# Triangular inverse of a chunked DeltaNet: the last doubling level as pairs of 64-row matmuls

## The chip, the cores and the metric

The kernel runs on 1 core of a Trainium2 chip. The metric is the device time of one launch in microseconds (us), the median of several runs. All data is fp32.

## What is computed

The reference is a two-layer encoder: a gated DeltaNet mixer, a latent attention mixer, and a mixture of experts behind each. The change is in the DeltaNet mixer. It has 8 key heads with 2 value heads each, 512 tokens, and runs the gated delta rule in both directions d (forward, and backward over flipped tokens). In each chunk it inverts a triangular matrix:

```python
a = jnp.where(strict, jnp.einsum('nbhcd,nbhsd->nbhcs', k_beta, k) * decay, 0.0)
t_inv = lax.linalg.triangular_solve(a + eye, jnp.broadcast_to(eye, a.shape),
                                    left_side=True, lower=True, unit_diagonal=True)
u = jnp.einsum('nbhcs,nbhsd->nbhcd', t_inv, v * beta[..., None])
w = jnp.einsum('nbhcs,nbhsd->nbhcd', t_inv, k_beta * jnp.exp(g)[..., None])
```

A recurrence over the chunks follows (`step` in the reference), then a norm, a gate and the output projection.

## The kernel before

The DeltaNet phase loops over the 8 key heads: `body` runs seven times in a hardware loop with the preparation of the next head woven in (`with_next`), and once more for the last head without it. A chunk is 128 tokens here, a tile of 128 x 128; there are TT = 4 tiles and two value heads h, so one fp32 bank of 128 x 512 holds the four tiles of one h.

The inverse is built by doubling. Diagonal blocks of 8 are solved first (L1027 to L1038). Then levels l = 3 to 6 merge blocks of size b = 2^l into blocks of 2b, for both directions at once: `TU[:, 0]` holds the transposed inverse T and `TU[:, 1]` the inverse U, each with a copy for direction 0 and one for direction 1, and `merged` (L287) reads them as one matrix whose column blocks alternate between the directions. At each level, for each value head h:

- TensorE makes X = A^T T (`make_x`, L550) in bank 4 + h, four 128 x 128 matmuls.
- VectorE masks the bank to the off-diagonal blocks of the level and writes it to `X` (`mask_x`, L1020), signalling `xm_ready`. `X` and `A` lie in the buffer that the profile calls `wd`.
- ScalarE copies U in merged order to `W` (L764), signalling `W_ready`.
- TensorE makes Y (`make_y`, L556, not at the last level) and V (`make_v`, L562) in banks 6 + h and 2 + h.
- VectorE subtracts them from T and U (`update`, L1025), signalling `T_ready` and `U_ready`.

Every engine follows its own instruction order, written out by hand; semaphores tie them together. TensorE puts `filler` pieces between these steps: in the loop heads 32 single matmuls of the next head's projections (L419), of which 8 stand ahead of the 8-blocks, 14 among them, and two at each of the two places of a level until they are used up; in the last head 16 pieces of the z projection. VectorE puts convolution steps (L930) and silu steps (L939) of the next head into numbered slots (`between`), four slots a level. At level 6 these are one convolution step between the two masks and one silu between the two updates.

Behind the last level TensorE runs the first quarter of the z projection (`make_z`, L503, only in the loop heads), and then the recurrence, whose first matmul L602 waits for all updates of U.

Of the kernel before, what the change touches and what calls it, by code (L numbers as in the profile page):

```python
# [7 lines left out]
ALU = mybir.AluOpType  # L8
# [4 lines left out]
P = 128  # L13
D = 1024
SEQ = 512
TT = SEQ // P
# [10 lines left out]
LEVELS, BASE = 7, 3  # L27
NL = LEVELS - BASE
# [87 lines left out]
PREPARE = [("D0", 2), ("tr0", 4), ("tr1", 5), ("tr2", 6), ("tr3", 7), ("D1", 3)]  # L116
TURN_O = [("oT0", 0), ("oT1", 1)]
PREPARE_LATE = [("kT", 2), ("qT", 3), ("KK", 2), ("KQ", 3)]


def dn_uses(with_next):
# [31 lines left out]
def delta_net(nc, t, dram):  # L153
# [4 lines left out]
    c, ps, res, xT = t["const"], t["ps"], t["res"], t["xT"]  # L158
# [5 lines left out]
    with ExitStack() as ctx:  # L164
# [12 lines left out]
        A, X = (t["wd"][:, 1, f].rearrange("p (c t n) -> p c t n", c=2, t=TT) for f in range(2))  # L177
# [11 lines left out]
        TU = sb("TU", [P, 2, 2, 2, TT, P])  # L189
        W = sb("W", [P, 2, TT, P])  # L190
# [30 lines left out]
        T_ready, U_ready = sem("T_ready"), sem("U_ready")  # L221
# [5 lines left out]
        xm_ready, W_ready = sem("xm_ready"), sem("W_ready")  # L227
# [8 lines left out]
        rows = Arrival(nc, t, sb, sem, 0)  # L236
# [144 lines left out]
        def _(pe):  # L381
# [13 lines left out]
            for n in range(8):  # L395
# [6 lines left out]
                for k in range(4):  # L402
                    mm = pe.transpose(ps[b][:, k * P:(k + 1) * P], res[:, tt, (half * 4 + k) * P:(half * 4 + k + 1) * P], ident)
# [4 lines left out]
            for tt in range(TT):  # L408
                for k in range(KD):
                    mm = pe.matmul(ps[2][:, tt * 64:(tt + 1) * 64], xT[:, k, tt * P:(tt + 1) * P], wba[:, k], start=k == 0, stop=k == KD - 1)  # L410
# [82 lines left out]
            def body(i, uses, with_next):  # L493
# [24 lines left out]
                def filler(n=1):  # L518
                    for _ in range(n):
                        if fill:  # L520
                            f, a = fill.pop(0)
                            f(*a)
# [4 lines left out]
                for m in range(7):  # L527
                    pe.wait_ge(R_ready, i * 8 + m + 1)
                    bank = begin(uses, f"B{m}", i)
# [23 lines left out]
                def make_y(l, h):  # L553
                    bank = begin(uses, f"Y{l}{h}", i)
                    for tt in range(TT):
                        mm = pe.matmul(bank[:, tt * P:(tt + 1) * P], W[:, h, tt], X[:, h, tt], start=True, stop=True)  # L556
                    done(mm, uses, f"Y{l}{h}")
# [4 lines left out]
                        mm = pe.matmul(bank[:, tt * P:(tt + 1) * P], X[:, h, tt], W[:, h, tt], start=True, stop=True)  # L562
                    done(mm, uses, f"V{l}{h}")

                for l in range(BASE, LEVELS):
                    make_x(l, 0)
                    make_x(l, 1)
                    filler(2 if with_next else 1)
                    for h in range(2):
                        pe.wait_ge(xm_ready, i * 2 * NL + 2 * (l - BASE) + h + 1)  # L570
                        pe.wait_ge(W_ready, i * 2 * NL + 2 * (l - BASE) + h + 1)
                        if l < LEVELS - 1:
                            make_y(l, h)
                        make_v(l, h)
                    filler(2 if with_next else 1)
                filler(99)

                if with_next:
# [289 lines left out]
        def _(dve):  # L868
# [8 lines left out]
            def got(uses, name, i):  # L877
                b, n = nth(uses, name, i)
                dve.wait_ge(full[b], n + 1)
                return ps[b]  # L880
# [118 lines left out]
            def body(i, uses, with_next, per):  # L999
# [15 lines left out]

                def mask_x(l, h):
                    bank = got(uses, f"X{l}{h}", i)
                    at = C_LEV + (l - BASE) * P
                    m = c[:, at:at + P].rearrange("p (o a) -> p o a", o=1).to_broadcast([P, TT, P])
                    nc.vector.tensor_tensor(X[:, h], bank[:].rearrange("p (t n) -> p t n", t=TT), m, ALU.mult).then_inc(xm_ready, 1)  # L1020

                def update(which, l, h):
                    bank = got(uses, f"{'YV'[which]}{l}{h}", i)
                    change = bank[:].rearrange("p (a e b) -> p a e b", e=2, b=1 << l)
                    nc.vector.tensor_tensor(merged(which, h, l), merged(which, h, l), change, ALU.subtract).then_inc(U_ready if which else T_ready, 1)  # L1025

# [1306 lines left out]
```

## Time and profile before

| | us |
|---|---|
| median of 3 runs | 1757.55 (1756.84 to 1757.8) |
| the profiled execution, its own time | 1760.1 |
| its span, first to last instruction | 1758.2 |
| TensorE busy (matmul) in it | 1576.9 |
| VectorE busy | 858.9 |
| ScalarE busy | 344.1 |
| GpSimd busy | 170.6 |
| mean granted TensorE clock | 0.948 |

One execution was taken by the profiler; its engines' rows give start, duration, engine, source line and tile names of each instruction. PE is TensorE's matmuls, PEld its weight loads, DVE VectorE, ACT ScalarE, POOL GpSimd, SP SyncE. An fp32 matmul of the program shows as two matmul records and two weight loads. A matmul's duration holds its latency, so the distance between starts, not the duration, is what one costs in a dense row. The 40 slices of the page are 44 us each.

### The profile page before, as it was taken

Reading aid. Unit: us, or ns where it says so; the run is one execution under the profiler, and the core shown is the slowest. Engines: PE = TensorE matmul, PEld = TensorE weight load, DVE = VectorE, ACT = ScalarE, POOL = GpSimd, SP = SyncE. Lnnn points to the kernel's source line nnn. Section 1 sums busy time; section 2 is a strip of 40 time slices with the busy share of each in tenths; the row PEclk is TensorE's granted clock in tenths of the full one; section 3 lists DMA queues with packets and bytes.
Section 4 is the critical chain, followed back from the end, with each engine's and each line's share of the span. In section 5 each row is a group of like instructions: output and inputs, shape, how many; then the busy total and the mean of one; then the engine's idle time right before and its main releaser. Section 6 shows DMA issues by size and latency. Waiting matters only on the chain. (4 is left out here: it accounts for less than half of the span.)

```text
span 1758.2 us, 20456 instructions
## 1 busy us (share of the span) xinstructions
PE 1576.9 (90%) x6926; PEld 995.4 (57%) x6926; DVE 858.9 (49%) x1768; ACT 344.1 (20%) x765; POOL 170.6 (10%) x171
## 2 busy tenths in 40 slices
PE   8899999999999999999986999937899997799990
PEld 5576685776857768577765444415555554644440
DVE  2665655656556565674566311134245557311115
ACT  2122122221212312222121111102322221111110
POOL 1201203012030120301101100020000001100002
PEclk9999999999999999999986999978899998699995
DMA  6760101101011010100510799932021133299964
GB/s 198 244 187 25 48 24 50 45 24 48 24 48 48 24 48 24 48 0 24 192 49 24 260 343 353 331 123 91 33 60 42 37 128 136 97 297 352 352 207 153
DMA packets 148743, 212.69 MB, mean 121 GB/s; under 512 B 8553, under 2 KB 120417, under 8 KB 148705
## 3 DMA queue, kind: packets, MB, share of 16 engines
q1 hardware_dynamic: 137600, 172.62, 30.3%
q10 hardware_dynamic: 6496, 22.81, 3.5%
q0 software_dynamic: 4608, 16.78, 2.6%
q8 instruction: 21, 0.34, 0.1%
q14 instruction: 18, 0.14, 0.0%
HBM read 174.96 MB, written 37.22 MB: 121 GB/s over the span
## 5 line engine op out<-in xcount | busy, mean ns | idle before, releaser
L1486 PE MATMUL bank<-wgu,moe_xgT 128*96 128x512 f32 x512 | 225.2, 592 | 4.3 <-DVE moe_xgT L1690 2.4
L419 PE MATMUL bank<-xT,wgu 128*128 128x512 f32 x448 | 210.6, 600 | 0.0
L1486 PEld LDWEIGHTS bank<-wgu,moe_xgT 128*96 128x96 f32 x512 | 80.9, 163 | 124.1 <-issue 124.1
L1690 DVE COPY moe_xgT<-bank 128x384 f32<-128x384 f32 x34 | 19.0, 558 | 209.8 <-PE bank L1474 205.6
L503 PE MATMUL bank<-wd,xT 128*128 128x256 f32 x512 | 117.7, 380 | 0.9 <-DVE res L1125 0.9
L1506 PE MATMUL bank<-wd,moe_hidT 128*96 128x512 f32 x256 | 115.3, 593 | 2.9 <-DVE moe_hidT L1698 2.9
L637 PE MATMUL bank<-wd,oT 128*128 128x512 f32 x256 | 116.3, 604 | 1.0 <-ACT oT L807 1.0
L419 PEld LDWEIGHTS bank<-xT,wgu 128*128 128x128 f32 x448 | 78.1, 191 | 63.7 <-issue 63.6
L503 PEld LDWEIGHTS bank<-wd,xT 128*128 128x128 f32 x512 | 95.7, 190 | 13.9 <-issue 1.7
L930 DVE SCALAR_TENSOR_TENSOR wgu<-bank,taps,wgu 128x510 f32<-128x510 f32 (+1 forms) x128 | 95.3, 744 | 8.6 <-ACT wgu L696 8.1
L1025 DVE TENSOR_TENSOR TU<-TU,bank 128x512 f32<-128x512 f32 x112 | 75.1, 686 | 20.5 <-PE bank L556 12.8
L637 PEld LDWEIGHTS bank<-wd,oT 128*128 128x128 f32 x256 | 48.3, 194 | 56.6 <-issue 52.2
L562 PE MATMUL bank<-W,wd 128*128 128x128 f32 x512 | 69.0, 278 | 7.1 <-DVE wd L1020 6.4
L1125 DVE TENSOR_TENSOR res<-res,bank 128x512 f32<-128x512 f32 x64 | 43.7, 686 | 56.6 <-PE bank L637 56.4
L1506 PEld LDWEIGHTS bank<-wd,moe_hidT 128*96 128x96 f32 x256 | 39.2, 163 | 54.7 <-issue 54.7
L562 PEld LDWEIGHTS bank<-W,wd 128*128 128x128 f32 x512 | 62.1, 192 | 9.8 <-DVE wd L1020 9.7
L550 PEld LDWEIGHTS bank<-TU,wd 128*128 128x128 f32 x512 | 62.0, 192 | 7.7 <-issue 6.7
L148 POOL TENSOR_TENSOR rs<-ss,masks 128x4 f32<-128x4 f32 x16 | 6.2, 387 | 616.4 <-DVE ss L1064 616.4
L550 PE MATMUL bank<-TU,wd 128*128 128x128 f32 x512 | 64.3, 278 | 0.0
L1547 ACT COPY moe_xgT<-bank 128x384 f32<-128x384 f32 x34 | 16.3, 478 | 242.8 <-PE bank L1474 208.0
L1704 DVE COPY moe_y_rows<-bank 96x512 f32<-96x512 f32 x32 | 22.0, 687 | 82.3 <-PE bank L1506 82.3
L1020 DVE TENSOR_TENSOR wd<-bank,masks 128x512 f32<-128x512 f32 x64 | 44.1, 689 | 36.7 <-PE bank L550 34.9
(308 smaller groups left out, 2468.3 us busy)
## 6 DMA issues: line engine op xcount, KB each, us to landing
wgu<-moe_w_gate SPq DMA_DIRECT2D x32, 1024.0 KB, 10.2
wgu<-moe_w_up SPq DMA_DIRECT2D x32, 1024.0 KB, 12.3
wd<-moe_w_down SPq DMA_DIRECT2D x32, 1024.0 KB, 5.8
wgu<-dn_w_in SPq DMA_DIRECT2D x32, 512.0 KB, 3.8
slots_y<-moe_y_rows ACTq DMA_DIRECT2D x32, 384.0 KB, 6.4
slots_x<-gains SPq DMA_DIRECT2D x1, 9984.0 KB, 39.2
moe_x_rows<-slots_x ACTq DMA_DIRECT2D x26, 384.0 KB, 7.7
wd<-dn_w_in SPq DMA_DIRECT2D x8, 1024.0 KB, 5.2
```

Source lines behind the costliest of these rows:

```text
L419: mm = pe.matmul(bank[:], wqkv[:, ct, k], xT[:, k], start=k == 0, stop=k == KD - 1)
L503: mm = pe.matmul(bank[:, (n % 2) * 256:(n % 2) * 256 + 256], xT[:, k, tt * P:(tt + 1) * P], wz[:, k], start=k == 0, stop=k == KD - 1)
L550: mm = pe.matmul(bank[:, tt * P:(tt + 1) * P], A[:, h, tt], merged(0, h, l, tt), start=True, stop=True)
L562: mm = pe.matmul(bank[:, tt * P:(tt + 1) * P], X[:, h, tt], W[:, h, tt], start=True, stop=True)
L637: mm = pe.matmul(bank[:], oT[:, h, tt], wo[:, h, half * 512:(half + 1) * 512], start=h == 0, stop=h == 1)
L930: ins = nc.vector.scalar_tensor_tensor(out=conv[:, ct, lo:hi], in0=bank[:, lo + d:hi + d], scalar=w[:, j:j + 1], in1=conv[:, ct, lo:hi], o ...
L1020: nc.vector.tensor_tensor(X[:, h], bank[:].rearrange("p (t n) -> p t n", t=TT), m, ALU.mult).then_inc(xm_ready, 1)
L1025: nc.vector.tensor_tensor(merged(which, h, l), merged(which, h, l), change, ALU.subtract).then_inc(U_ready if which else T_ready, 1)
L1125: nc.vector.tensor_tensor(y, y, bank[:], ALU.add).then_inc(y_ready, 1)
L1486: mm = pe.matmul(ps[2][0:CAP], xgT[:, r, k], wgu[:, r, k].rearrange("p a f -> p (a f)"), start=k == 0, stop=k == KD - 1)
L1506: mm = pe.matmul(ps[4 + half][0:CAP], hidT[:, f], wd[:, r, f, half * 512:(half + 1) * 512], start=f == 0, stop=f == 1)
L1704: nc.vector.tensor_copy(y_rows[:, r, 512:1024], ps[5][0:CAP]).then_inc(y_ready[1], 1)
```

## The change

At level 6 the blocks are 64 wide, and of each direction only one corner of a tile is missing. The change makes just that corner. X and V of the last level become 16 matmuls of 64 rows x 64 columns each (weights 64 x 128) instead of 8 per product of 128 x 128, alternating between the two directions: direction 0 reads partitions 0 to 63 and writes bank 4 (X) or 2 (V), direction 1 reads 64 to 127 and writes bank 5 or 3. A bank now belongs to a direction and holds both value heads, eight groups of 64 columns. The mask becomes a copy of 64 partitions, and the update of U touches the corner alone. X waits for all updates of T of level 5, V for both copies and both parts of W.

```diff
--- before.py
+++ after.py
@@ -116,6 +116,9 @@
 PREPARE = [("D0", 2), ("tr0", 4), ("tr1", 5), ("tr2", 6), ("tr3", 7), ("D1", 3)]
 TURN_O = [("oT0", 0), ("oT1", 1)]
 PREPARE_LATE = [("kT", 2), ("qT", 3), ("KK", 2), ("KQ", 3)]
+
+
+HALVES = slice(0, P // 2), slice(P // 2, P)
 
 
 def dn_uses(with_next):
@@ -562,17 +565,40 @@
                         mm = pe.matmul(bank[:, tt * P:(tt + 1) * P], X[:, h, tt], W[:, h, tt], start=True, stop=True)
                     done(mm, uses, f"V{l}{h}")
 
-                for l in range(BASE, LEVELS):
+                def last_x():
+                    l = LEVELS - 1
+                    pe.wait_ge(T_ready, i * (2 * NL - 2) + (l - BASE) * 2)
+                    banks = [ps[uses.at[f"X{l}{h}"][0]] for h in range(2)]
+                    for n in range(2 * TT):
+                        for d, rows in enumerate(HALVES):
+                            mm = pe.matmul(banks[d][:, n * 64:n * 64 + 64], A[rows, n // TT, n % TT], TU[rows, 0, d, n // TT, n % TT, rows], start=True, stop=True)
+                            if n == 2 * TT - 1:
+                                done(mm, uses, f"X{l}{d}")
+
+                def last_v():
+                    l = LEVELS - 1
+                    pe.wait_ge(xm_ready, (i + 1) * 2 * NL)
+                    pe.wait_ge(W_ready, (i + 1) * 2 * NL)
+                    banks = [ps[uses.at[f"V{l}{h}"][0]] for h in range(2)]
+                    for n in range(2 * TT):
+                        for d, rows in enumerate(HALVES):
+                            mm = pe.matmul(banks[d][:, n * 64:n * 64 + 64], X[rows, n // TT, n % TT], W[rows, n // TT, n % TT, rows], start=True, stop=True)
+                            if n == 2 * TT - 1:
+                                done(mm, uses, f"V{l}{d}")
+
+                for l in range(BASE, LEVELS - 1):
                     make_x(l, 0)
                     make_x(l, 1)
                     filler(2 if with_next else 1)
                     for h in range(2):
                         pe.wait_ge(xm_ready, i * 2 * NL + 2 * (l - BASE) + h + 1)
                         pe.wait_ge(W_ready, i * 2 * NL + 2 * (l - BASE) + h + 1)
-                        if l < LEVELS - 1:
-                            make_y(l, h)
+                        make_y(l, h)
                         make_v(l, h)
                     filler(2 if with_next else 1)
+                last_x()
+                filler(2 if with_next else 1)
+                last_v()
                 filler(99)
 
                 if with_next:
@@ -1015,12 +1041,21 @@
 
                 def mask_x(l, h):
                     bank = got(uses, f"X{l}{h}", i)
+                    if l == LEVELS - 1:
+                        rows, other = HALVES[h], HALVES[1 - h]
+                        nc.vector.tensor_copy(X[other].rearrange("p h t n -> p (h t) n")[:, :, rows], bank[other].rearrange("p (g n) -> p g n", n=64)).then_inc(xm_ready, 1)
+                        return
                     at = C_LEV + (l - BASE) * P
                     m = c[:, at:at + P].rearrange("p (o a) -> p o a", o=1).to_broadcast([P, TT, P])
                     nc.vector.tensor_tensor(X[:, h], bank[:].rearrange("p (t n) -> p t n", t=TT), m, ALU.mult).then_inc(xm_ready, 1)
 
                 def update(which, l, h):
                     bank = got(uses, f"{'YV'[which]}{l}{h}", i)
+                    if l == LEVELS - 1:
+                        rows, other = HALVES[h], HALVES[1 - h]
+                        corner = TU[other, 1, h].rearrange("p h t n -> p (h t) n")[:, :, rows]
+                        nc.vector.tensor_tensor(corner, corner, bank[other].rearrange("p (g n) -> p g n", n=64), ALU.subtract).then_inc(U_ready, 1)
+                        return
                     change = bank[:].rearrange("p (a e b) -> p a e b", e=2, b=1 << l)
                     nc.vector.tensor_tensor(merged(which, h, l), merged(which, h, l), change, ALU.subtract).then_inc(U_ready if which else T_ready, 1)
```

On TensorE, at level 6 of a loop head, before (names: `TU` is T, `wd` holds A and X, `W` the merged U; the first rows end level 5):

```order
L562 MATMUL bank<-W,wd 128x128 [waits U_ready]
L562 MATMUL bank<-W,wd 128x128 x3
L547 REGISTER_ALU
L550 MATMUL bank<-TU,wd 128x128 [waits xm_ready,T_ready]
L550 MATMUL bank<-TU,wd 128x128 x3
...
L562 MATMUL bank<-W,wd 128x128 [waits U_ready,W_ready,xm_ready]
L562 MATMUL bank<-W,wd 128x128 x3
L579 REGISTER_ALU
L386 REGISTER_ALU [waits z_in]
L503 MATMUL bank<-wd,xT 128x256 [waits conv_ready]
```

The rows left out are the second value head's X and the first one's V, with waits of their own. The same place now:

```order
L565 MATMUL bank<-W,wd 128x128 [waits U_ready]
L565 MATMUL bank<-W,wd 128x128 x3
L570 REGISTER_ALU
L574 MATMUL bank<-TU,wd 128x64 [waits T_ready]
L574 MATMUL bank<-TU,wd 128x64 x15
L580 ISA
L585 MATMUL bank<-W,wd 128x64 [waits W_ready,xm_ready]
L585 MATMUL bank<-W,wd 128x64 x15
L605 REGISTER_ALU
L389 REGISTER_ALU [waits z_in]
L506 MATMUL bank<-wd,xT 128x256 [waits conv_ready]
```

Two waits for T and two for the masked X have become one each, ahead of twice as many matmuls. No other work of TensorE has moved.

On VectorE, at level 6 of a loop head, before (`bank` of the first row is X of value head 0; L930 is the convolution, L939 the silu):

```order
L1020 TENSOR_TENSOR wd<-bank,masks 128x512 [waits dn_full4]
L930 SCALAR_TENSOR_TENSOR wgu<-bank,taps,wgu 128x510
L879 REGISTER_ALU
L1020 TENSOR_TENSOR wd<-bank,masks 128x512 [waits dn_full5]
L879 REGISTER_ALU
L1025 TENSOR_TENSOR TU<-TU,bank 128x4x2x64 [waits dn_full2]
L938 REGISTER_ALU
L939 SCALAR_TENSOR_TENSOR wgu<-wgu 128x512 [waits th_ready]
L1025 TENSOR_TENSOR TU<-TU,bank 128x4x2x64 [waits dn_full3]
```

And now:

```order
L1046 COPY wd<-bank 64x8x64 [waits dn_full4]
L956 SCALAR_TENSOR_TENSOR wgu<-bank,taps,wgu 128x510
L905 REGISTER_ALU
L1046 COPY wd<-bank 64x8x64 [waits dn_full5]
L905 REGISTER_ALU
L1057 TENSOR_TENSOR TU<-TU,bank 64x8x64 [waits dn_full2]
L964 REGISTER_ALU
L965 SCALAR_TENSOR_TENSOR wgu<-wgu 128x512 [waits th_ready]
L1057 TENSOR_TENSOR TU<-TU,bank 64x8x64 [waits dn_full3]
```

The order and the banks waited for are the same; the tiles have half the partitions and as many elements in each.

## Rows read from the trace of the kernel before

**Rows 1.** Page: TensorE's busy time, and the granted clock in 40 slices, tenths.
```profile
PE 1576.9 (90%) x6926; PEld 995.4 (57%) x6926; DVE 858.9 (49%) x1768; ACT 344.1 (20%) x765; POOL 170.6 (10%) x171
...
PEclk9999999999999999999986999978899998699995
```

**Rows 2.** Timeline of level 6, second head: start, us, engine, line, tiles, count, [idle <-releaser].
```profile
227.91 1.06 PE L562 MATMUL bank<-W,wd 128*128 128x128 f32 x8
...
228.81 2.10 PE L550 MATMUL bank<-TU,wd 128*128 128x128 f32 x16
229.01 1.28 DVE L1025 TENSOR_TENSOR TU<-TU,bank 128x512 f32<-128x512 f32 x2
230.21 0.74 DVE L930 SCALAR_TENSOR_TENSOR wgu<-bank,taps,wgu 128x511 f32<-128x511 f32 x1
...
231.08 0.69 DVE L1020 TENSOR_TENSOR wd<-bank,masks 128x512 f32<-128x512 f32 x1
231.68 0.74 DVE L930 SCALAR_TENSOR_TENSOR wgu<-bank,taps,wgu 128x510 f32<-128x510 f32 x1
...
231.82 2.41 PE L562 MATMUL bank<-W,wd 128*128 128x128 f32 x16 [0.91 <-DVE wd L1020]
232.34 0.68 DVE L1020 TENSOR_TENSOR wd<-bank,masks 128x512 f32<-128x512 f32 x1
...
233.08 0.97 PEld L562 LDWEIGHTS bank<-W,wd 128*128 128x128 f32 x8 [0.29 <-DVE wd L1020]
...
234.07 3.62 PE L503 MATMUL bank<-wd,xT 128*128 128x256 f32 x16
...
237.53 0.94 PE L602 MATMUL bank<-v,TU 128*128 128x128 f32 x7
```

**Rows 3.** Timeline of level 6 in the last head.
```profile
882.87 0.69 DVE L1025 TENSOR_TENSOR TU<-TU,bank 128x512 f32<-128x512 f32 x1 [0.21 <-PE bank L556]
...
883.56 1.95 PE L550 MATMUL bank<-TU,wd 128*128 128x128 f32 x16
...
888.24 0.49 PE L602 MATMUL bank<-v,TU 128*128 128x128 f32 x2 [0.78 <-DVE TU L1025]
```

**Rows 4.** Instructions by line and shape: count, busy us, mean ns, idle before.
```profile
L1020 DVE TENSOR_TENSOR wd<-bank,masks 128x512 f32<-128x512 f32 x64 | 44.1, 689 | 36.7 <-PE bank L550 34.9
...
L2250 DVE COPY mla_pT<-bank 128x512 f32<-128x512 f32 x16 | 11.1, 692 | 22.1 <-PE bank L2061 22.0
...
L410 PE MATMUL bank<-wba,xT 128*128 128x64 f32 x64 | 7.3, 275 | 0.8 <-ACT xT L673 0.8
```

**Rows 5.** Timeline of the attention's 64-row pairs (L2051) between full matmuls.
```profile
1268.18 1.88 PE L2048 MATMUL bank<-mla_knT,mla_qnT 128*128 128x512 f32 x4
...
1269.99 0.30 PEld L2051 LDWEIGHTS bank<-mla_krT,mla_qrT 64*128 64x128 f32 x4 [0.76 <-issue]
1269.99 1.13 PE L2051 MATMUL bank<-mla_krT,mla_qrT 64*128 64x512 f32 x4
...
1271.05 0.30 PEld L2048 LDWEIGHTS bank<-mla_knT,mla_qnT 128*128 128x128 f32 x2 [0.76 <-issue]
```

**Rows 6.** Stretches A:B: length, busy time of each engine, PEclk, DMA share, GB/s.
```profile
63.00:66.30 3.30, 3.30 (x16) 2.97 (x15) 0.77 (x2) 0.99 (x3) 0.00 (x0) 0.50 1.06 353
...
228.80:234.10 5.30, 4.29 (x35) 3.83 (x34) 5.14 (x9) 1.41 (x3) 0.00 (x0) 1.00 0.05 7
...
1254.50:1257.50 3.00, 1.85 (x18) 1.76 (x16) 0.00 (x0) 1.17 (x4) 0.00 (x0) 1.00 0.00 0
1257.60:1264.30 6.70, 6.70 (x16) 3.78 (x15) 1.75 (x6) 0.00 (x0) 0.00 (x0) 0.50 0.00 0
```

**Rows 7.** Timeline of TensorE around gaps: the clock held, fell, fell.
```profile
56.44 1.44 PE L470 MATMUL bank<-masks,wgu 128*128 128x128 f32 x8 [1.99 <-DVE wgu L939]
...
62.02 1.46 PE L481 MATMUL bank<-masks,kq 128*128 128x128 f32 x8 [2.42 <-DVE kq L965]
...
1255.77 3.69 PE L2015 MATMUL bank<-mla_wq,mla_cqT 128*128 128x64 f32 x24 [1.15 <-ACT mla_ckvT L2135]
```

## The prediction

> **What bounds the kernel now.** The page comes first: TensorE is busy for 1576.9 us, 90% of the span, and the whole delta-net phase but its start runs at the full granted clock [rows 1]. Whatever lengthens TensorE's own path in the delta-net phase lengthens the kernel. The timeline around the last doubling level of one loop head says what counts there [rows 2]. Read it engine by engine. L562 of level 5 starts its last group at 227.91; L550 of level 6 follows at 228.81 without a gap. L550 takes 2.10 us, where 16 such records take 1.95 [rows 3]: its second half waits for level 5's third update (the first of the pair L1025 at 229.01). TensorE then has nothing until 231.82: no projection filler is left by level 6 (32 pieces of k, gone by level 5), and the mask L1020 starts only at 231.08, behind a convolution step L930. One mask, a convolution (231.68) and the other mask (232.34) later L562 has done both halves, and at 234.07 L503, the z projection, starts: 16 records, 3.62 us. It covers the updates of U behind V, for L602, which waits for them, starts at 237.53 with no idle time in front of it. So in a loop head the time between the end of level 5 and L503 (228.81 to 234.07) is on the path, and the updates behind it are not. In the last head there is no z projection behind V and no convolution step between the masks: L602 waits for the last update (0.78 us idle) [rows 3].
>
> **How one fp32 product is paid.** Every matmul of the program leaves two records, two passes. For 128 columns a pass takes 0.89 / 8 = 0.11 us (L562 at 227.91 to L550 at 228.81) [rows 2]. A pass that moves only 64 columns takes as long: L410 is 64 passes of 64 columns in 7.3 us, 0.114 each [rows 4]. The weight load of 128 columns sets it, not the columns moved. So halving the columns alone gains nothing, and the program now issues 32 small matmuls a head at this level where it had 16.
>
> **Do the pairs overlap?** The nearest rows are L2051, 64-row matmuls in pairs on opposite halves [rows 5]. Two of them, four passes of 512 columns, start at 1269.99 and the next full one follows at 1271.05: 1.06 us, where four passes of L2048 need 4 x 0.43. All four weight loads lie within 0.30 us, where each takes 0.18. Both halves load and stream together. At the borders the loads cannot run ahead: 0.76 us between loads where 0.24 is usual, and about 0.1 us lost on each side. I take this: 8 pairs x 2 passes x 0.111 = 1.78 us for X and as much for V, just what the 16 full passes take now, plus 0.11 for the first load. The other end, no overlap, is 32 x 0.114 = 3.65 us each. The Trainium skill (TensorEngine Tiling (Array Packing), sections "Theoretical Speedup" and "Key Properties") promises up to 2x for each small dimension and says that changing the mode drains the engine. The trace agrees on the drain, about 0.1 us; the first promise would make a stage of 64 rows and 64 columns faster than today's, and is rival D.
>
> **The change part by part, one loop head.**
> (1) X now waits for both halves of T before its first matmul. Level 5's third update starts at 229.01 and takes 0.69; a waiting weight load starts 0.06 behind its releaser (232.34 + 0.68 to 233.08 for L562) [rows 2]. X starts at 229.75 instead of 228.81: 0.94 us of idle TensorE, of which the old order lost 0.15 in L550.
> (2) X ends at 229.75 + 0.11 + 1.78 = 231.64. A consumer sees a group about 0.2 us after its last pass (L562 at 227.91, eight passes, L1025 at 229.01). Both banks are finished together, so the first mask cannot start before about 231.80; it started at 231.08.
> (3) The masks become copies of 64 partitions x 512 elements. An instruction of VectorE is paid by elements per partition; a copy of 512 from a bank is 692 ns against 689 for L1020 [rows 4]. No gain. The convolution step stays between them. From first mask to the second's release takes 0.60 + 0.66 + 0.74 = 2.00 us as now, but V needs both copies, since each half of the partitions reads what the other bank gave. V starts at 233.80, where V of half 0 started at 231.82.
> (4) V ends at 233.80 + 0.11 + 1.78 = 235.69, and leaving the 64-row mode costs 0.1 + 0.1: L503 stands 1.8 us later than 234.07.
> (5) The updates: two of 512 elements per partition, 0.69 each with the silu between, done by about 237.8. L503 runs until 239.5 and hides them. If that cover were gone they would cost 2.2 us. ScalarE's W copies follow level 5's updates, which are unmoved, and are done before V asks. SyncE's weight issue behind the convolution moves by 0.7 us and is wanted only in the next head.
> Seven loop heads: 7 x 1.8 = 12.6 us.
> (6) The last head: third update ends 883.56, X 883.61 to 885.50, masks from 885.66 at a pitch of 0.60, V from 887.0 to 888.89, updates from 889.05 to 890.34, L602 at 890.40 where it stood at 888.23 [rows 3]: 2.2 us.
> Without the clock the sum is 14.8 us.
>
> **The clock.** This is the unknown cost, and the choice that moves the number most. The granted clock is 1.00 (2.4 GHz) through level 6 now, with 4.29 of 5.30 us busy and 128 columns a pass [rows 6]. It fell to 0.50 (1.2 GHz) in two places that look like the new level 6 [rows 6, 7]: after 2.42 us idle and L481 (0.50 over 63.0 to 66.3), and, the closest, after 1.15 us idle and 1.85 us of L2015's 64-column passes, with a granted clock of 0.50 over 1257.6 to 1264.3. It held over the 1.99 us gap of L470, between dense 128-column passes. The new level 6 is 0.94 us idle, 1.9 us of 64-column passes, 2.15 us idle (231.65 to 233.80), 1.9 us of 64-column passes: longer and thinner than the stretch at 1254.5 to 1257.5. I expect a fall in nearly every head. The price is half of the busy time at the low clock: a short low stretch (3.3 us, as at 63.0) loses 1.7 us, a long one (6.7 us, as at 1257.6) 3.4. As V itself is thin, like L2015 there, I take 3.4 for the seven heads and 1.7 for the last: 23.8 + 1.7 = 25.5 us. The bounds are 0 and 3.4 in all eight, 27. The Trainium skill (TensorE: Matmul & The Clock Gate, section "Why this matters for your kernels") ties a fall to idle gaps longer than any worked out here; by it alone nothing falls, which is rival B.
>
> **The sum.** 14.8 + 25.5 = 40.3 us, on the profiled execution's own 1760.1 us: 1800.4. The median of the runs, 1757.55, lies 2.55 below that: 1798 us.
>
> **The rivals.**
> A, the forecast: pairs overlap and the clock falls at level 6. 1798, with 1785 (1.7 us in each head, 1757.5 + 14.8 + 13.6) and 1806 as its ends. Chance 0.55.
> B: pairs overlap, the clock holds, because both halves stream at once and count for more than one thin pass. 1757.5 + 14.8 = 1772. For it: slices 3 to 20 of the page, the loop heads with their gaps of 0.91 us, never fell [rows 1]. Against: L2015 [rows 7]. Chance 0.25.
> C: the 64x128 pairs with 64 columns do not overlap, as each half's stream is shorter than its load and L2051 shows only long streams. Twice 1.87 us more a head, 8 x 3.7 = 30: 1802, and up to 1828 with the clock. Chance 0.12.
> D, the other side: a 64-row weight load is cheap when paired, and passes are paid by their columns, 0.056 us. X and V then take 0.9 us each, 1.8 less a head, which just pays (1) to (4): 1757.5 + 14.8 - 8 x 1.8 = 1758, no change; it would be faster from 0.05 a pass on. Against: in L2051 the second loads come 0.11 us behind the first, as at full width. Chance 0.05.
> The remaining 0.03 is a mistake of mine in the waits, either way.
>
> **How the numbers follow.** The likeliest is A, 1798. From 1769 (below B) to 1808 (above A) the range holds A, B and a third of C, about 0.84; its lower end is B's with 3 us less for the DVE pitch of (3). About 0.2% (3.5 us) is what a measurement of this kernel can tell from no change. Faster 0.02, same 0.05, slower 0.93: the first two are D and half of the remainder.
>
> **What would show it.** X's 32 records should last 1.9 us from the first to the last (C: 3.6; D: 0.9); 0.9 us idle in front of X, about 2.1 in front of V, and L503 some 1.8 us later behind level 5 at the full clock; low digits in the page's row of granted clock in slices 3 to 20, and low stretches that begin at level 6. If the low stretches are missing, A is wrong and B right. If V starts before both copies end, or L602 waits for an update in a loop head, the waits are misread.

## The result and the profile after

The changed kernel takes 1801.58 us (median of 4 runs, 1797.7 to 1805.1) against 1757.67: 43.9 us more, a ratio of 1.0249 (95% interval 1.0223 to 1.0276). It is slower, inside the range of 1769 to 1808 and 3.6 us above the forecast of 1798. The profiled execution took 1804.2 us, with a span of 1802.3 and a mean granted clock of 0.932, where the one before had a span of 1758.2 and 0.948.

Level 6 of the second head again, start, us, engine, line, tiles, count, [idle before <-releaser]. It answers to [rows 2]; L574 is the new X, L585 the new V, L1046 the copy, L1057 the corner's update, L506 the z projection, L628 the recurrence:

```profile
234.65 1.06 PE L565 MATMUL bank<-W,wd 128*128 128x128 f32 x8
...
235.74 1.28 DVE L1060 TENSOR_TENSOR TU<-TU,bank 128x512 f32<-128x512 f32 x2
...
236.49 2.00 PE L574 MATMUL bank<-TU,wd 64*128 64x64 f32 x32 [0.78 <-DVE TU L1060]
...
238.52 0.69 DVE L1046 COPY wd<-bank 64x512 f32<-64x512 f32 x1 [0.83 <-PE bank L574]
239.25 0.75 DVE L956 SCALAR_TENSOR_TENSOR wgu<-bank,taps,wgu 128x510 f32<-128x510 f32 x1
239.91 0.67 DVE L1046 COPY wd<-bank 64x512 f32<-64x512 f32 x1
...
240.64 3.07 PE L585 MATMUL bank<-W,wd 64*128 64x64 f32 x32 [2.15 <-DVE wd L1046]
...
243.64 5.94 PE L506 MATMUL bank<-wd,xT 128*128 128x256 f32 x16
243.74 0.69 DVE L1057 TENSOR_TENSOR TU<-TU,bank 64x512 f32<-64x512 f32 x1 [3.15 <-PE bank L585]
...
245.18 0.68 DVE L1057 TENSOR_TENSOR TU<-TU,bank 64x512 f32<-64x512 f32 x1
...
249.42 1.05 PE L628 MATMUL bank<-v,TU 128*128 128x128 f32 x8
```

Read behind the end of level 5 (L565's last group starts at 234.65 and streams 0.89 us, so 235.54; in [rows 2] 228.81):

| us behind level 5 | before | forecast without the clock | after |
|---|---|---|---|
| X starts | 0 | 0.94 | 0.95 |
| first mask or copy starts | 2.27 | 2.99 | 2.98 |
| V starts | 3.01 | 4.99 | 5.10 |
| z projection starts | 5.26 | 7.1 | 8.10 |

Up to V's start the waits come as worked out. From there V's 32 records take 3.07 us where X's 32 records of the same shape take 2.00, and the z projection's 16 records 5.94 us where they took 3.62. The granted clock fell to 0.50 meanwhile; that the fall is the cause is tested below. Stretches A:B of the changed kernel: length, TensorE busy (records), granted clock, DMA share, GB/s. One low stretch (clock 0.50) lies at level 6 of each of the eight heads:

```profile
122.00:132.00 10.00, 8.60 (x44) 0.50 0.49 135
241.40:248.00 6.60, 6.60 (x34) 0.50 0.29 78
357.50:364.10 6.60, 6.60 (x37) 0.50 0.29 81
473.60:480.20 6.60, 6.60 (x40) 0.50 0.31 81
589.60:596.20 6.60, 6.56 (x39) 0.50 0.29 81
705.70:712.30 6.60, 6.43 (x39) 0.50 0.30 81
821.70:828.30 6.60, 6.28 (x38) 0.50 0.00 0
924.10:934.10 10.00, 8.37 (x48) 0.50 0.28 105
1586.30:1589.50 3.20, 3.20 (x4) 0.50 1.08 385
```

The kernel before had none in its loop heads: the stretch at level 6 in [rows 6] stands for all seven of its loop heads. The last row of the stretches is a fall in the second mixture of experts, whose code the change does not touch. In four of the seven loop heads the fall came before V had started: V's first records stand at 123.40, 589.64, 705.87 and 822.02 us, so there it was the idle time behind the thin passes of X in which the clock fell. In the other three it came 0.1 to 0.7 us into V. The page shows less of all this than the stretches do, since a slice of 45 us averages over a fall of 7 (a 9 means 0.9 or more), and the low digits that the prediction named as a sign are, in the loop heads, a single 8:

```profile
PEclk9989999999999999999988799986899999699995
```

Of the 44.1 us between the two spans, 42.5 are lost in the delta-net phase: the first transposes of the next phase stand at 929.4 before and 971.9 after. The other 1.6 come later, where the fall at 1586.3 is what the kernel before did not have.

```profile
L1251 PE MATMUL bank<-masks,res x64: 272/421/476, 929.4 to 1500.1; 128*128 128x128 f32 x64
```

After:

```profile
L1286 PE MATMUL bank<-masks,res x64: 272/421/477, 971.9 to 1542.3; 128*128 128x128 f32 x64
```

### The profile page after: what moved, and what is told of

The parts are those of the page before. It is cut to its first block and busy times, and to the rows that moved or that the text cites. A ratio compares the mean times of both kernels' runs of the same rounds, so it can differ in the third digit from the quotient of the medians.

```text
span 1802.3 us, 20944 instructions
## 1 busy us (share of the span) xinstructions
PE 1604.0 (89%) x7182; PEld 1019.8 (57%) x7182; DVE 860.7 (48%) x1768; ACT 343.9 (19%) x765; POOL 169.7 (9%) x171
## 5 line engine op out<-in xcount | busy, mean ns | idle before, releaser
L506 PE MATMUL bank<-wd,xT 128*128 128x256 f32 x512 | 131.1, 411 | 0.9 <-DVE res L1160 0.9
L506 PEld LDWEIGHTS bank<-wd,xT 128*128 128x128 f32 x512 | 105.0, 209 | 18.1 <-issue 1.7
L1060 DVE TENSOR_TENSOR TU<-TU,bank 128x512 f32<-128x512 f32 x96 | 64.1, 686 | 20.0 <-PE bank L559 12.8
L817 ACT ACTIVATE vs<-bank,gb 128x128 f32<-128x128 f32 x96 | 30.4, 374 | 175.4 <-PE bank L628 175.1
L722 ACT ACTIVATE wgu<-bank,taps 128x512 f32<-128x512 f32 x28 | 19.2, 687 | 203.4 <-PE bank L422 203.4
L876 POOL TENSOR_TENSOR qkd<-wgu 128x512 f32<-128x512 f32 x32 | 47.6, 1517 | 106.1 <-DVE wgu L1003 106.1
L559 PEld LDWEIGHTS bank<-wd,W 128*128 128x128 f32 x384 | 48.6, 192 | 10.2 <-issue 10.0
L1860 POOL DMA_INDIRECT moe_fetched<-slots_y,moe_place x16 | 17.9, 1117 | 378.8 <-PEq L1849 374.5
## 6 DMA issues: line engine op xcount, KB each, us to landing
wgu<-moe_w_up SPq DMA_DIRECT2D x32, 1024.0 KB, 12.4
```

What stands on the lines that cost most here:

```text
L506: mm = pe.matmul(bank[:, (n % 2) * 256:(n % 2) * 256 + 256], xT[:, k, tt * P:(tt + 1) * P], wz[:, k], start=k == 0, stop=k == KD - 1)
L817: ins = act.mul(vs[:, d, h], bank[:, h * P:(h + 1) * P], gb[:, COEF * TT + tt, d, h:h + 1])
L876: nc.gpsimd.tensor_tensor(qkd[:, 2 * d + h], dec[:, h], kqm[:, d], ALU.mult).then_inc(qkd_ready, 1)
```

## The experiments

Nine kernels were run, each with runs of the kernel before beside it. Every ratio below is to those.

| kernel | median, us | before beside it | ratio (95%) | recurrence starts | heads with a fall |
|---|---|---|---|---|---|
| before | 1757.67 | | 1 | 8.72 | 0 of 7 |
| the change | 1801.58 | 1757.67 | 1.0249 (1.0223 to 1.0276) | 13.6 to 14.8 | 7 of 7 |
| dense work ahead of V | 1777.04 | 1756.49 | 1.0116 (1.0100 to 1.0133) | 10.59; 11.93 with a fall | 2 of 7 |
| T in halves | 1792.99 | 1756.49 | 1.0210 (1.0193 to 1.0227) | 11.5 to 13.2 | 7 of 7 |
| V alone in pairs | 1788.91 | 1756.49 | 1.0183 (1.0166 to 1.0200) | 11.4 to 13.1 | 7 of 7 |
| waits only | 1766.51 | 1756.49 | 1.0052 (1.0036 to 1.0069) | 9.80 | 0 of 7 |
| V waits for both masks | 1772.15 | 1760.54 | 1.0066 (1.0045 to 1.0086) | 9.77; 11.2 to 11.4 with a fall | 3 of 7 |
| z in the gap, full matmuls | 1753.74 | 1760.0 | 0.9966 (0.9956 to 0.9976) | 7.86 | 0 of 7 |
| pairs, z in the gaps | 1772.43 | 1760.0 | 1.0072 (1.0057 to 1.0086) | 9.32 | 0 of 7 |
| quadrants | 1765.44 | 1760.0 | 1.0034 (1.0020 to 1.0048) | 8.32; 9.9 with a fall | 2 of 7 |
| quadrants, z in the gaps | 1747.9 | 1760.0 | 0.9923 (0.9910 to 0.9936) | 6.73 | 0 of 7 |

The fifth column gives the first matmul of the recurrence in a loop head, in us behind the end of level 5, and the last one the loop heads whose granted clock fell at level 6, both from the profiled execution. The kernel before took 1756.49 to 1760.54 us on the chips used, up to 4 us apart, so results are given below as a difference to the runs beside them, and expectations, which are times beside 1757.6, likewise. A pass is one matmul record. Thin passes move 64 columns, dense ones 128 or more. Each kernel was profiled once, so counts of heads are counts in one execution.

**Is it the clock? Dense work ahead of V.** The changed kernel with matmuls of no use between X and V.

```diff
+                def busy(n):
+                    for _ in range(n):
+                        pe.matmul(ps[6][:], ident, xT[:, 0], start=True, stop=True)
...
                 last_x()
+                busy(2 if with_next else 1)
                 last_v()
```

> The changed kernel, with dense matmuls of no use (identity times 512 columns of xT, two in a loop head, one in the last, 0.86 us each, into bank 6, which nothing uses then) in TensorE's idle time between X and V. Their sum, 1.7 us, is less than the 2.26 us for which TensorE stood idle there, so V should start where it did. Theory (waits plus clock): the clock stays at its upper level at level 6, V takes 1.9 us instead of up to 3.4 and the z projection 3.5 instead of 5.5: about 1773 us, 1.85 us a loop head above the kernel before. Rival (the pairs of V are slow in themselves, for example because the two halves get in each other's way, and the clock record only accompanies it): V stays at 3.4 us and the time at 1800 or above.

Measured: 1777.04 us, 20.5 above before where 15 was expected, and less than half of the 43.9 of the change. Timeline of TensorE in its third head (L591 is the work of no use, L633 the recurrence's first matmul):

```profile
343.39 1.06 PE L565 MATMUL bank<-W,wd 128*128 128x128 f32 x8
345.23 2.00 PE L574 MATMUL bank<-TU,wd 64*128 64x64 f32 x32 [0.78 <-DVE TU L1065]
347.16 1.99 PE L591 MATMUL bank<-xT,masks 128*128 128x512 f32 x4
349.38 2.00 PE L585 MATMUL bank<-W,wd 64*128 64x64 f32 x32 [0.24 <-DVE wd L1051]
351.32 3.72 PE L506 MATMUL bank<-wd,xT 128*128 128x256 f32 x16
354.87 1.05 PE L633 MATMUL bank<-v,TU 128*128 128x128 f32 x8
```

Level 5 ends at 344.28. X starts at 0.95 and V at 5.10, exactly where they start in the changed kernel, but V now takes 2.00 us, just as X, and the z projection 3.72. The rival that the pairs of V are slow in themselves falls: adding work to TensorE took 23 us off. In five loop heads the clock stays up and the recurrence starts at 10.59. In two it fell 0.2 and 0.3 us after the dense work had begun (at 233.0 and 799.6 us), and the work itself ran slow. Those two, 1.3 us later each, and a low stretch of 3.4 us in the last head, at the recurrence's start, make up most of the 5 us above the expectation. Stretches (length, busy, granted clock, DMA share, GB/s); the first row is of the third head, which has no fall, the other two of the second, before and in the fall:

```profile
344.30:354.80 10.50, 9.48 (x86) 1.00 0.18 51
229.90:233.00 3.10, 2.32 (x35) 1.00 0.00 0
233.10:236.30 3.20, 3.20 (x4) 0.50 0.13 32
```

So a loop head without a fall costs 10.59 - 8.72 = 1.87 us more than before, and in the changed kernel the fall costs the rest.

**Is it the wait for T? T in halves.** X starts with the first value head's T.

```diff
-                    pe.wait_ge(T_ready, i * (2 * NL - 2) + (l - BASE) * 2)
+                    pe.wait_ge(T_ready, i * (2 * NL - 2) + (l - BASE) * 2 - 1)
...
                     for n in range(2 * TT):
+                        if n == TT:
+                            pe.wait_ge(T_ready, i * (2 * NL - 2) + (l - BASE) * 2)
```

> The changed kernel, but X starts its first eight pairs (value head 0) when T of value head 0 is there and waits for the other only ahead of its ninth pair. Theory: X starts 0.95 us earlier and ends about 0.9 earlier; the first copy is then held by VectorE's convolution step until 2.3 us behind level 5, so V starts at about 4.3 instead of 5.1 in a loop head: 0.75 us less in each. The clock still falls, since idle time and thin passes in front of V are the same: about 1795 us. If the joined wait for T were most of the loss, the time would come below 1785.

Measured: 1792.99 us, 36.5 above before (37 expected). V starts at 4.39 behind level 5 (expected 4.3), and a low stretch remains in all seven loop heads. That the joined wait for T is most of the loss, which would have given 27 or less, is out. The joined wait for T is worth 0.7 us a head before the clock is counted, and 7.4 us in all.

**Which waits, which shape? The waits only.** The kernel before, full matmuls, with both waits joined as in the change.

```diff
                 for l in range(BASE, LEVELS):
+                    if l == LEVELS - 1:
+                        pe.wait_ge(T_ready, i * (2 * NL - 2) + (l - BASE) * 2)
                     make_x(l, 0)
...
+                    if l == LEVELS - 1:
+                        pe.wait_ge(xm_ready, (i + 1) * 2 * NL)
+                        pe.wait_ge(W_ready, (i + 1) * 2 * NL)
                     for h in range(2):
```

> The kernel before with nothing but the two joined waits: X of level 6 waits for both halves of T, V for both masks and both parts of W; all matmuls full, 128 x 128. Theory: X starts at 0.95, ends at 2.73; V starts at about 4.3 (second mask) and ends at 6.05: 0.8 us a loop head, 1.0 in the last. The passes are dense and the idle times 0.95 and 1.5 us, so the clock holds: about 1764 us. If the idle time alone brings the clock down, 1775 or more.

Measured: 1766.51 us, 10.0 above before where 6.4 was expected. The clock held in every loop head, through two idle times (L550 is X, L562 V, L607 the recurrence):

```profile
229.54 2.02 PE L550 MATMUL bank<-TU,wd 128*128 128x128 f32 x16 [0.99 <-DVE TU L1030]
232.89 2.02 PE L562 MATMUL bank<-W,wd 128*128 128x128 f32 x16 [1.33 <-DVE wd L1025]
234.75 3.62 PE L503 MATMUL bank<-wd,xT 128*128 128x256 f32 x16
238.21 1.05 PE L607 MATMUL bank<-v,TU 128*128 128x128 f32 x8
```

The recurrence starts at 9.80, 1.08 later than before (0.8 expected: both waits ended 0.2 us later than the timeline of before suggested). In the seven heads that is 2.0 us above the expectation. The other 1.6 are lost in the last head, far ahead of its level 6, where the granted clock was 0.50 from 858.1 to 861.4 us and the kernel before has no such stretch. So of the 1.87 us that a head without a fall costs, about 1.1 are the waits, and 0.8 the pairs. No run takes these 0.8 apart; likely parts are that both banks of X finish together and that the engine leaves the 64-row mode in front of z.

**V alone in pairs.** X and its masks as before, V as in the change.

```diff
-                last_x()
+                make_x(LEVELS - 1, 0)
+                make_x(LEVELS - 1, 1)
...
                 last_v()
...
                     bank = got(uses, f"X{l}{h}", i)
-                    if l == LEVELS - 1:
-                        rows, other = HALVES[h], HALVES[1 - h]
...
-                        return
```

> X of the last level made and masked as before, V alone as 64-row pairs with its wait for both halves of X. Theory: V starts at about 4.3 us behind level 5 (second mask), ends at 6.1, z at 6.3 where it stood at 5.27: 1.0 us a loop head without the clock. TensorE stands idle for 2.3 us in front of thin passes, so the clock falls in most heads and adds 1.7 to 3.4 us each: 1778 to 1792 us. If only X's and V's thin passes together bring the clock down, 1766 us.

Measured: 1788.91 us, 32.4 above before, at the upper end of the 20 to 34 that the theory gave, and not the 8 of the case in which only X and V together bring the clock down. All seven loop heads have a low stretch, and in each it begins in V, 0.4 to 1.7 us behind its start. Thin passes of X are therefore not needed for a fall. TensorE in the second head:

```profile
231.49 2.10 PE L553 MATMUL bank<-TU,wd 128*128 128x128 f32 x16
235.76 2.67 PE L585 MATMUL bank<-W,wd 64*128 64x64 f32 x32 [2.17 <-DVE wd L1047]
238.36 6.36 PE L506 MATMUL bank<-wd,xT 128*128 128x256 f32 x16
244.55 1.05 PE L629 MATMUL bank<-v,TU 128*128 128x128 f32 x8
```

**Idle time or thin passes? V waits for both masks.** Nearly the same idle time ahead of V, 2.35 us for 2.17, but dense 128-column passes behind it: of the waits-only kernel the second edit alone.

> The kernel before with one joined wait: V of level 6 waits for both masks and both parts of W; all matmuls full. In a loop head TensorE should be idle from 1.94 to 4.27 us behind level 5, as in the run with V alone in pairs, but dense 128-column passes follow in place of thin ones. Theory (it is idle time and thin passes together that bring the clock down): V from 4.27 to 6.1, 0.8 us a loop head, and falls in fewer heads than the seven there: 0 to 3 of 7, 1764 to 1770 us. Rival (the 2.3 us of idle time are enough by themselves): a fall in nearly every head, 1775 or more.

Measured: 1772.15 us, 11.6 above before, inside the 6 to 12 of the theory and below the 17 of the rival. The trace says the same: a fall in three of seven loop heads, where V in pairs had seven of seven. TensorE in the fourth head, one of the three (V at 457.29 takes 3.58 us for its 16 records instead of 2.02):

```profile
452.84 2.10 PE L550 MATMUL bank<-TU,wd 128*128 128x128 f32 x16
457.29 3.58 PE L562 MATMUL bank<-W,wd 128*128 128x128 f32 x16 [2.35 <-DVE wd L1023]
460.70 3.62 PE L503 MATMUL bank<-wd,xT 128*128 128x256 f32 x16
```

The fall itself, as a stretch (length, busy, granted clock, DMA share, GB/s):

```profile
457.20:460.40 3.20, 3.11 (x14) 0.50 0.62 167
```

In this execution idle time between dense passes was enough in some heads, and with thin passes behind it in all. The falls also differ in length: here all three last 3.4 us, with V in pairs five of seven last 6.8 us. Which of the heads fall when the shape is the same was not settled: the idle time is 2.35 us in all seven. Nor was X in pairs with V in full matmuls run, the shape that would show what the thin passes of X do by themselves.

**Filling the gaps with work that is needed.** If idle TensorE ahead of V is the trouble, the z projection, which stands right behind V and waits for nothing, can fill it. First with the pairs as they are:

```diff
+                if with_next:
+                    pe.wait_ge(z_in, (i + 1) * 16)
+                    make_z(0, (0, 2))
                 last_x()
+                if with_next:
+                    make_z(0, (2, 6))
                 last_v()
...
-                        make_z(step)
+                        make_z(step, (0 if step else 6, KD))
```

> The changed kernel, row pairs as they are, but with six of the eight matmuls of the first z quarter in its gaps: two in front of X (0.9 us, gap 0.95), four between X and V (1.8 us, gap 2.3). Theory: the clock holds in the loop heads, V starts at 5.1 as before; the first matmul of the recurrence then waits for the last update, at about 9.3 us behind level 5, where the kernel before has 8.7: 0.6 us a loop head, and the last head unchanged with its fall, 2 to 4 us: 1764 to 1767 us. Rival (64-row passes bring the clock down whatever lies beside them): 1785 or more.

Measured: 1772.43 us, 12.4 above before where 6 to 9 was expected. In the loop heads all is as expected: no fall, V at 5.11, the recurrence at 9.32 after a wait for the last update, 4.2 us in the seven. The rival that 64-row passes bring the clock down whatever lies beside them is out: the same pairs as in the change, with z in their gaps, went without a fall in seven of seven. The last head has no z projection to fill with: it lost 4.1 us up to the recurrence, as in the change. Of the rest, 1.4 us are lost between the start of the last head's recurrence and the next phase, as in the change, and a low stretch in the second mixture of experts is a part, which the kernel before did not have there (length, TensorE busy, granted clock, DMA share, GB/s):

```profile
1539.90:1543.10 3.20, 3.20 (x5) 0.50 0.95 379
```

TensorE in the second head (L506 is z, L629 the recurrence):

```profile
228.75 1.03 PE L506 MATMUL bank<-wd,xT 128*128 128x256 f32 x4
229.71 2.00 PE L574 MATMUL bank<-TU,wd 64*128 64x64 f32 x32
231.64 1.99 PE L506 MATMUL bank<-wd,xT 128*128 128x256 f32 x8
233.86 2.00 PE L585 MATMUL bank<-W,wd 64*128 64x64 f32 x32 [0.23 <-DVE wd L1047]
235.79 1.13 PE L506 MATMUL bank<-wd,xT 128*128 128x256 f32 x4
238.07 1.16 PE L629 MATMUL bank<-v,TU 128*128 128x128 f32 x8 [1.15 <-DVE TU L1058]
```

Then with the kernel before, no pairs at all, two z matmuls between X and V of level 6:

> The kernel before, full 128 x 128 matmuls throughout, but the first two of the eight matmuls of the first z quarter (0.9 us) are done between X and V of level 6, where TensorE stood idle for 0.91 and 0.29 us; the other six stay behind V. Theory: nothing waits for the z quarter there, V still starts with its masks, and the z part behind V is 0.9 us shorter: 0.85 us less a loop head, about 1751 us. Rival (the idle time in front of V costs nothing, since something else sets the head's end): 1757.

Measured: 1753.74 us, 6.3 below before (6.6 expected), 0.34% faster. The recurrence (L602) starts at 7.86 to 7.87, 0.86 earlier, in every loop head, as expected. TensorE in the second head (level 5 ends at 227.07):

```profile
229.01 1.03 PE L503 MATMUL bank<-wd,xT 128*128 128x256 f32 x4
230.08 2.42 PE L562 MATMUL bank<-W,wd 128*128 128x128 f32 x16
...
234.93 1.05 PE L602 MATMUL bank<-v,TU 128*128 128x128 f32 x8
```

**Quadrants.** The pairs load 128 columns of weights and need 64. Here each half of a pair is a 64 x 64 corner of the array, and the two write opposite halves of one bank, so that a single copy moves both corners. A 64 x 128 matmul whose result is not used stands in front of each group and carries its wait (of X's here).

```diff
+                    bank = ps[uses.at[f"X{l}0"][0]]
+                    pe.matmul(ps[5][:, 0:64], A[HALVES[0], 0, 0], TU[HALVES[0], 0, 0, 0, 0, HALVES[0]], start=True, stop=True)
                     for n in range(2 * TT):
                         for d, rows in enumerate(HALVES):
-                            mm = pe.matmul(banks[d][:, n * 64:n * 64 + 64], A[rows, n // TT, n % TT], TU[rows, 0, d, n // TT, n % TT, rows], start=True, stop=True)
+                            other = HALVES[1 - d]
+                            mm = pe.matmul(bank[other, n * 64:n * 64 + 64], A[rows, n // TT, n % TT, other], TU[rows, 0, d, n // TT, n % TT, rows], start=True, stop=True)
...
+                        nc.vector.tensor_copy(X[:, 0].rearrange("p t n -> p (t n)"), bank[:]).then_inc(xm_ready, 2)
```

> The changed kernel with the weights of the pairs cut to the 64 columns that are needed, so that each pair is two 64 x 64 corners of the array which write opposite halves of one bank. One copy of 128 partitions then moves both corners of X, and V waits for one copy instead of two. A 64 x 128 matmul of no use carries each wait. Theory: a pass is paid by its weight load, 64 columns 0.056 us, so X and V take 1.1 us instead of 1.84; V starts at about 3.1 instead of 5.1, and without the clock the loop head would be 0.9 us shorter than before the change. TensorE is busier by nothing, so the clock falls as in the changed kernel and adds 1.7 to 3.4 us a head: 1765 to 1778. If 64-column loads are no faster, X and V stay at 1.8 and the time is 1775 or more.

Measured: 1765.44 us, 5.4 above before where 7 to 20 was expected, 38 less than the change. The expectation took a fall for granted in every head. TensorE in the fourth head (L575 and L587 are the matmuls that carry the waits; 64*64 is the shape of the weights):

```profile
452.33 1.06 PE L568 MATMUL bank<-W,wd 128*128 128x128 f32 x8
454.17 0.43 PE L575 MATMUL bank<-TU,wd 64*128 64x64 f32 x2 [0.78 <-DVE TU L1066]
454.53 1.15 PE L579 MATMUL bank<-TU,wd 64*64 64x64 f32 x32
456.54 0.43 PE L587 MATMUL bank<-W,wd 64*128 64x64 f32 x2 [0.86 <-DVE wd L1052]
456.90 1.15 PE L591 MATMUL bank<-W,wd 64*64 64x64 f32 x32
457.98 3.72 PE L509 MATMUL bank<-wd,xT 128*128 128x256 f32 x16
```

32 records of 64 x 64 take 1.15 us where the 64 x 128 ones take 2.00, with as many rows and moved columns: the weight load was the price of a pass, and half its columns cost little more than half. The clock fell in two of seven loop heads only. The idle times are shorter, 0.78 and 0.86 us by the rows, where the change had 0.78 and 2.15; whether that is the reason was not tested apart.

With two z matmuls ahead of X, two between X and V, and the last silu behind the last update:

> The same quadrants, with two matmuls of the z quarter in front of X and two between X and V, and the silu of slot 22 moved behind the last update. Theory: the clock holds, V starts at about 3.1 us behind level 5 and ends at 4.2, the last update at 5.9, the z rest (four matmuls, 1.8 us) at 6.1: 2.5 us a loop head less than the kernel before has. About 1740 us. If the clock still falls in most heads, 1755.

Measured: 1747.9 us, 12.1 below before where 17.6 was expected: 0.77% faster than the kernel before, and by the two ratios 3.2% faster than the change. The recurrence starts at 6.73, 2.0 earlier than before where 2.5 was expected. V starts at 3.8 instead of 3.1: the matmul that carries a wait costs 0.36 us (454.17 to 454.53 above) in front of X and again in front of V, which the expectation left out. No loop head has a fall.

## Why the prediction was right

**The bound.** Right. TensorE's path between level 5 and the recurrence sets the end: what the recurrence's start lost in the eight heads adds up to 40.5 us (36.4 in the loop heads, 4.1 in the last) of the 42.5 by which the next phase starts later.

**Pairs overlap, parity at best.** Right: X's 32 records take 2.00 us, where 16 full ones take 1.95 [rows 3]; the trace of L2051 [rows 5] was the right row to read. Rival C (3.6 us) is out, and so is D (0.9): in the changed kernel a pass is paid by its 128-column load. A thin pass became cheaper only with the quadrants, where the load itself is halved.

**Steps (1) to (4), the waits.** Right in place and size: 1.8 us a head forecast, 1.87 measured where no clock stands in the way. Step (3) was 0.1 short (2.12 from the first copy to V, not 2.00). Step (5), the cover of z over the updates, held: in the change L628 never waited for an update in a loop head.

**Step (6), the last head.** Forecast 2.2 us and 1.7 for the clock; measured 4.1 up to the recurrence. The low stretch there lasts 10 us instead of the short one assumed and runs 4.8 us into the recurrence.

**What no term covers.** The profiled execution came 3.8 us above the 1800.4 of the sum. The seven loop heads account for none of it (12.6 + 23.8 = 36.4 forecast, 36.4 measured), the last head up to the recurrence for 0.2. The other 3.6 lie elsewhere: 0.7 ahead of the first head's level 6, 1.3 between the start of the last head's recurrence and the next phase, and 1.6 in the later phases. That they are small beside the range is luck, not working.

**The clock.** Right, and the largest term: 23.8 us forecast for the seven loop heads (3.4 each). Measured: the recurrence starts 5.2 us later on average (36.4 / 7), less the 1.87 without a fall is 3.3 us a head, 23.3 in all. A low stretch of 6.6 to 10 us lies in every one. The choice of the long stretch, because V itself is thin, was the one that put the number within 4 us: the short one gives 1785. The runs bear it out, with long stretches in all seven heads of the change, and in five of seven with V alone in pairs, and short ones in all three falls of the kernel with full matmuls. One thing in the forecast was misplaced: in four loop heads the clock was down before V began. What the prediction read from L2015 [rows 7], that idle time with thin passes brings a fall, was confirmed by three kernels: one in which dense work took most falls away, and two in which nearly the same idle time was followed by thin or by dense passes. The row itself was weaker than it was taken for, since the granted clock had been 0.50 from 1247.4 to 1254.2 us, just ahead of it, and no fall in a loop head has such a stretch ahead of it. Rival B, by which the clock holds, is refuted by the falls in all eight heads. By the Trainium skill (TensorE: Matmul & The Clock Gate, section "Why this matters for your kernels"), with idle gaps as short as these the clock should have held. The traces do not agree: gaps of 0.95 and 2.15 us with 64-column passes between them were enough seven times of seven, and one of 2.35 us between dense passes three times of seven.

**What was missed.** The runs of the changed kernel spread over 7.4 us, those of before over 1.7. Of the kernels that shared one set of runs, the quadrants, in which only some heads fall, spread most, 13.8 us over 10 runs (1757.57 to 1771.39), where the kernel before spread 4.9 over 23. Each run also has its mean granted clock on record, and the two go together: the quadrants have 0.948 in the fastest run and 0.939 in the slowest, with the others in order between, and the change 0.935 at 1797.7 us and 0.930 at 1805.1. So the spread goes with the clock. That it is the number of falls at level 6 which differs is likely but was not shown, since only one execution of each was profiled.

## What to carry to other kernels

Before shrinking a matmul, read from the trace what a pass is paid by: here it was the weight load, so fewer rows and fewer moved columns gained nothing, and only fewer weight columns made the group of passes shorter. A change that makes TensorE's work thinner and lets it wait can cost more by the clock than by the wait, here 3.3 us a head against 1.87. Look at the granted clock of the stretch and not of the page, and fill the gap with work that is due anyway: two z matmuls in the gap made the kernel before 6.3 us faster with no change of the inverse at all. Joining two waits into one makes the first half wait for the second half's releaser: price it by what stands between the two on the engine that releases them.

## What the runs showed of the hardware

- Two 64-row fp32 matmuls on opposite halves of the partitions run side by side also when each moves only 64 columns: 32 passes take 2.00 us where one after the other they would take 3.65, about 0.115 a pair (V, start to the start of z, 1.94 us in the kernel with dense work).
- Two 64 x 64 corners that write opposite halves of the same bank run side by side too, at 0.063 us a pair of passes (32 records in 1.15 us, latency taken off).
- The granted clock fell to 0.50 after 2.2 us idle followed by thin passes in 7 of 7 heads (V alone in pairs), after 2.35 us idle followed by dense passes in 3 of 7, and after 0.99 and 1.33 us of idle time between dense passes in none of 7. Thin passes with dense ones in their gaps did not bring it down (pairs with z in the gaps, 0 of 7), but thin passes behind 0.95 us idle, with dense ones from there on, did in 2 of 7 (dense work ahead of V).
- While the clock is low, passes that are paid by their weight load take nearly twice as long too: V's 32 records take 3.68 us where it fell ahead of V (the first head of the change, 123.40 us), and 2.00 at the full clock.
- Changing between full and 64-row matmuls costs about 0.1 us each way (pairs with z in the gaps: four z records in front of X take 0.96 us from start to start, where 16 in a row in [rows 2] take 3.46), and a 64 x 128 matmul that only carries a wait 0.36.
